# Expert 0's rows by one-hot products instead of a gather, in a mixer and MoE layer on one core

## The reference

```python
p_group = softmax(hf @ rg_w + rg_b)
g_prob, g_idx = top_k(p_group, 1)
top_p, top_i = top_k(softmax(sel), 2)
w = g_prob * top_p / sum(top_p)
for e in range(16):
    y = (silu(h @ w_gate[e]) * (h @ w_up[e])) @ w_down[e]
    out = out + combine[:, e:e + 1] * y
```

## Time and profile before

| | us |
|---|---|
| median of 3 runs | 552.3 (551.95 to 555.5) |
| the profiled execution | 552.4 |
| its span (first to last instruction) | 550.6 |
| TensorE busy in the span | 536.9 |
| VectorE / ScalarE / GpSimd busy | 421.3 / 353.3 / 91.3 |

### The profile page before, as it was taken

One profiled execution on the slowest core, in us unless ns is written; L12 is line 12 of the kernel. 1 busy time (PEld: TensorE's weight loads), 2 busy tenths in 40 slices (PEclk: granted clock), 3 DMA queues, 4 the chain that ended last, 5 costly groups with the idle time before them and its releaser, 6 DMA issues.

```text
span 550.6 us, 7873 instructions
## 1 busy us (share of the span) xinstructions
PE 536.9 (98%) x2662; PEld 438.5 (80%) x2663; DVE 421.3 (77%) x580; ACT 353.3 (64%) x470; POOL 91.3 (17%) x113
## 2 busy tenths in 40 slices
PE   7999999999999999999999999999999999999995
PEld 5988777777877888877788888888888888888883
DVE  5654599554864753588989898988989898988986
ACT  5563654780326253355778978788778978788745
POOL 3260000000000000031412222022212222110420
PEclk9999999999999999999999999999999999999998
DMA  8999122323020237639999999999999999999796
GB/s 322 371 283 401 42 71 77 76 79 77 0 77 0 78 114 251 234 138 313 349 380 373 379 394 382 367 371 376 392 352 374 375 390 373 376 390 393 251 208 212
DMA packets 63821, 144.03 MB, mean 262 GB/s; under 512 B 3833, under 2 KB 13361, under 8 KB 63665
## 3 DMA queue, kind: packets, MB, share of 16 engines
q1 hardware_dynamic: 56528, 120.24, 61.4%
q0 software_dynamic: 7120, 22.90, 13.7%
q10 hardware_dynamic: 144, 0.52, 0.3%
HBM read 132.77 MB, written 14.30 MB: 267 GB/s over the span
## 4 chain that ended last, share of the span: by engine, by line
PE 88%; DVE 5%; ACT 2%; DMA 2%; issue 1%; POOL 0%; DVEq 0%; POOLq 0%
PE ps L1495 25%; PE ps L1497 24%; PE ps L1496 24%; PE ps L1502 7%; PE ps L1646 2%; PE ps L1632 2%; PE ps L1608 1%; PE ps L1578 1%; PE ps L1673 1%; DMA arena<-h_dram,meta 1%; DMA arena<-norm_g 1%; DVE lo_ring L1305 1%; DVE act_lo L1015 1%; PE ps L1896 1%; DVE res L1474 0%
## 5 line engine op out<-in xcount | busy, mean ns | idle before, releaser
L1305 DVE TENSOR_TENSOR lo_ring<-arena,hi_ring 128x2048 fp32r<-128x2048 f32 x94 | 213.8, 2288 | 26.9 <-ACT hi_ring L894 26.8
L1495 PE MATMUL ps<-hi_ring,act_hi 128*128 128x512 f32 x576 | 229.8, 399 | 1.5 <-DVE lo_ring L1305 1.1
L1497 PE MATMUL ps<-hi_ring,act_lo 128*128 128x512 f32 x576 | 224.9, 390 | 0.0
L1496 PE MATMUL ps<-lo_ring,act_hi 128*128 128x512 f32 x576 | 224.4, 390 | 0.0
L894 ACT ACTIVATE hi_ring<-arena 128x2048 fp32r<-128x2048 f32 x94 | 180.2, 1917 | 28.1 <-PE ps L1497 28.1
L1495 PEld LDWEIGHTS ps<-hi_ring,act_hi 128*128 128x128 f32 x576 | 108.3, 188 | 23.5 <-issue 2.4
L1497 PEld LDWEIGHTS ps<-hi_ring,act_lo 128*128 128x128 f32 x576 | 108.1, 188 | 23.3
L1496 PEld LDWEIGHTS ps<-lo_ring,act_hi 128*128 128x128 f32 x576 | 108.4, 188 | 20.9
L1005 DVE SCALAR_TENSOR_TENSOR lo_ring<-arena,over,hi_ring 128x512 fp32r<-128x512 f32 x40 | 29.2, 747 | 29.4 <-ACT hi_ring L708 29.2
L1015 DVE TENSOR_TENSOR act_lo<-ps,act_hi 128x512 fp32r<-128x512 f32 x56 | 36.7, 683 | 7.6 <-ACT act_hi L742 5.6
L600 POOL DMA_INDIRECT arena<-h_dram,gather_idx x14 | 34.7, 2478 | 24.0 <-issue 24.0
(11 more groups left out here) (237 smaller groups left out, 523.0 us busy)
## 6 DMA issues: line engine op xcount, KB each, us to landing
arena<-w_gate SPq DMA_DIRECT2D x32, 1024.0 KB, 16.6
arena<-w_up SPq DMA_DIRECT2D x32, 1024.0 KB, 17.6
arena<-w_down SPq DMA_DIRECT2D x32, 1024.0 KB, 15.2
arena<-w_in SPq DMA_DIRECT2D x16, 512.0 KB, 7.2
y_dram<-arena POOLq DMA_DIRECT2D x8, 512.0 KB, 11.2
res<-y_dram POOLq DMA_DIRECT2D x8, 512.0 KB, 9.8
arena<-w_in SPq DMA_DIRECT2D x2, 1024.0 KB, 10.9
arena<-w_out SPq DMA_DIRECT2D x4, 512.0 KB, 6.5
```

Source lines behind the costliest of these rows:

```text
L1305: nc.vector.tensor_tensor(lo(N1 + n12), raw(n12), hi(N1 + n12).bitcast(F32), ALU.subtract).then_inc(lo_done, 1)
L1495: nc.tensor.matmul(dst, a_hi, b_hi, start=start, stop=False)
L1496: nc.tensor.matmul(dst, a_hi, b_lo, start=False, stop=False)
L1497: return nc.tensor.matmul(dst, a_lo, b_hi, start=False, stop=stop)
```

## The change

The normed tiles get homes of their own in SBUF (`h2_home`) and stay there. VectorE compares each token's rank in expert 0 with the row numbers (`find_first`), and TensorE multiplies each normed tile with that one-hot (`first_rows`): four f32 matmuls for each tile and half, summed over the four tiles in banks 4 and 5, which gives expert 0's rows turned. These take the place of expert 0's list, gather and transposes, and of the fillers. The lists are still made, for the other experts: GpSimd's first gathers are now those of experts 1 and 2, behind the last one-hot product, since two of the tiles lie in `x_rows`. The list's weights are made behind the first two products instead of before them. Differences and sums for the routing weights move from VectorE to GpSimd. Lengths, slots and flags move into VectorE's steps of experts 0 and 1. The two `y_buf` change places, so that `route` lies over `y_buf[1]`; ScalarE waits for the flags before expert 1's scaled rows instead of before the first silu. GpSimd waits for the lengths before its gather of expert 3. SyncE's loads 8 to 10 wait for the last h2 tile and the two turned halves.

```diff
-y_buf = [nc.alloc_sbuf_tensor_at("y0", [P, D], F32, offset=at_hi + 2560 * 4),
-         nc.alloc_sbuf_tensor_at("y1", [P, D], F32, offset=at_lo + 2560 * 4)]
+y_buf = [nc.alloc_sbuf_tensor_at("y0", [P, D], F32, offset=at_lo + 2560 * 4),
+         nc.alloc_sbuf_tensor_at("y1", [P, D], F32, offset=at_hi + 2560 * 4)]
...
-h2_buf = [region(O_XG, D), region(O_XG + D, D)]
+x_rows = [region(O_XG, D), region(O_XG + D, D)]
+h2_home = [region(O_BIAS, D), region(O_BIAS + D, D), x_rows[1], x_rows[0]]
+first_hot = region(O_BIAS + 2 * D, T * P).rearrange("p (t s) -> p t s", t=T)
...
-route = y_buf[0][:, 0:1024]
+route = y_buf[1][:, 0:1024]
...
-        if n == RING2 - 4:
-            sp.wait_ge(rows_in[0], 16)
+        if n == O_BIAS // GRAN - 1:
+            sp.wait_ge(h2_out[T - 1], 16)
+        elif n == O_BIAS // GRAN:
+            sp.wait_ge(x_turned, 1)
+        elif n == O_BIAS // GRAN + 1:
+            sp.wait_ge(x_turned, 2)
...
-        pool.dma_start(h2_dram[t * P:(t + 1) * P, :], h2_buf[t % 2]).then_inc(h2_out[t % 2], 16)
+        pool.dma_start(h2_dram[t * P:(t + 1) * P, :], h2_home[t]).then_inc(h2_out[t], 16)
...
+    pool_steps = [0]
...
+    def pool_done(ins):
...
+    g_top, g_exp = route[:, 472:472 + T], route[:, 848:864].rearrange("p (t j) -> p t j", t=T)
+    diff = route[:, 400:400 + T * E].rearrange("p (t g j) -> p t g j", t=T, g=N_GROUPS)
+    pool_done(nc.gpsimd.tensor_tensor(diff.rearrange("p t g j -> p (t g j)"), route[:, 704:768], route[:, 640:704], ALU.subtract))
+    pool_done(nc.gpsimd.tensor_tensor(diff, diff, lg[:, :, 1:, :], ALU.mult))
+    nc.gpsimd.tensor_tensor(g_exp, lg[:, :, 0, :], g_top.unsqueeze(2).to_broadcast([P, T, 4]),
+                            ALU.subtract).then_inc(pool_step, 1)
+    pool_steps[0] += 1
+    folded = diff.rearrange("p t g j -> p t (g j)")
+    for n in (8, 4, 2):
+        pool_done(nc.gpsimd.tensor_tensor(folded[:, :, 0:n], folded[:, :, 0:n], folded[:, :, n:2 * n], ALU.add))
+    nc.gpsimd.tensor_tensor(route[:, 864:868].unsqueeze(2), folded[:, :, 0:1], folded[:, :, 1:2], ALU.add).then_inc(gate_d, 1)
...
-    for b in range(2):
-        pool.wait_ge(h2_out[b], 16 * T // 2)
+    for t in range(T):
+        pool.wait_ge(h2_out[t], 16)
     pool.wait_ge(lists_ready, 1)
-    for b in range(2):
-        pool.indirect_dma_start(x_rows[b], None, h2_dram, bass.IndirectOffsetOnAxis(ap=meta[:, 4 * b:4 * b + 1], axis=0),
-                                bounds_check=last_token, oob_is_err=False).then_inc(rows_in[b], 16)
+    pool.wait_ge(x_turned, 2)
+    for e in (1, 2):
+        pool.indirect_dma_start(x_rows[e % 2], None, h2_dram, bass.IndirectOffsetOnAxis(ap=meta[:, 4 * e:4 * e + 1], axis=0),
+                                bounds_check=last_token, oob_is_err=False).then_inc(rows_in[e % 2], 16)
     pool.dma_start(gain2, bass.AP(final_g.tensor, 0, [[0, P], [1, D]])).then_inc(gain_in, 16)
-    pool.wait_ge(info_made, 1)
+    pool.wait_ge(lengths_made, 1)
...
     def gather(b, e):

         nc.gpsimd.tensor_copy(gather_idx[:, b:b + 1], meta[:, bass.ds(e * 4, 1)]).then_inc(idx_ready, 1)
-        pool.wait_ge(idx_ready, e - 1)
...
-    pool.wait_ge(x_turned, 2)
-    pool.wait_ge(rows_in[0], 16)
-    gather(0, 2)
     pool.wait_ge(y_zeroed, 16 * 2 * T)
     pool.wait_ge(x_turned, 4)
     pool.wait_ge(rows_in[1], 16)
     gather(1, 3)
+    pool.wait_ge(info_made, 1)
     for e in range(2):
         traffic(e, e, True, False)
...
-    act.wait_ge(gate_d, 1)
-    nc.scalar.activation(route[:, 848:868], route[:, 848:868], ACT.Exp).then_inc(gate_e, 1)
-    nc.scalar.activation(stat[:, 47:48], eps[:, 0:1], ACT.Silu)
...
         if not first:
             act.wait_ge(y_sent[b], e * 8 - 8 * b)
+        elif b:
+            act.wait_ge(over_set, 1)
...
     split(2, 2, 16)
-    rows_hi(0, 1)
+    nc.scalar.activation(stat[:, 46:47], eps[:, 0:1], ACT.Exp)
+    rows_hi(0, 1, (0,))
+    act.wait_ge(gate_d, 1)
+    nc.scalar.activation(route[:, 848:868], route[:, 848:868], ACT.Exp).then_inc(gate_e, 1)
+    rows_hi(0, 1, (1,))
+    nc.scalar.activation(stat[:, 47:48], eps[:, 0:1], ACT.Silu)
     split(3, 3, 16)
-    act.wait_ge(over_set, 1)
     act.wait_ge(mm_done, used_value(N1 + 1))
     nc.scalar.activation(silu_g[:, :], ps[:, 0, :], ACT.Silu).then_inc(silu_ready, 1)
...
-            act.wait_ge(y_sent[0], 16 * (E // 2 - 1))
+            act.wait_ge(y_sent[1], 16 * (E // 2 - 1))
...
-        if t >= 2:
-            dve.wait_ge(h2_out[t % 2], 16)
-        nc.vector.scalar_tensor_tensor(h2_buf[t % 2], res_t[:, t, :], rms[:, T + t:T + t + 1], gain2,
+        nc.vector.scalar_tensor_tensor(h2_home[t], res_t[:, t, :], rms[:, T + t:T + t + 1], gain2,
...
         nc.vector.tensor_scalar(pair_any[:, t0 * E:t1 * E], flat, 2.0, None, ALU.is_lt).then_inc(pair_ready, 1)
+        if t1 == T:
+            nc.vector.tensor_reduce(g_top, lg[:, :, 0, :], AX_X, ALU.max)
...
+    def find_first(t0, t1, ahead):
+
+        last = t1 == T
+        step_done(nc.vector.tensor_scalar(miss[:, t0:t1], standing[:, t0:t1, 0, 0], 2.0, 2.0 * S, ALU.is_ge, ALU.mult))
+        dve.wait_ge(rank_ready, 2 if last else 1)
+        step_done(nc.vector.tensor_tensor(first_rank[:, t0:t1], ahead, miss[:, t0:t1], ALU.add))
+        for t in range(t0, t1):
+            nc.vector.tensor_scalar(first_hot[:, t, :], order, first_rank[:, t:t + 1], None,
+                                    ALU.is_equal).then_inc(first_hot_set, 1)
...
+    find_first(0, EARLY, ps[:, 1, 0:EARLY * E:E])
     find_ranks(0, EARLY, ps[:, 1, 0:EARLY * E])
-    mark(0)
     norm2(T - 1)
     gate(EARLY, T)
-    mark(1)
+    find_first(EARLY, T, ps[:, 2, 0:(T - EARLY) * E:E])
     find_ranks(EARLY, T, ps[:, 2, 0:(T - EARLY) * E])
-    for t in range(EARLY, T):
+    for t in range(T):
         mark(t)
+    nc.vector.tensor_copy(count, ps[:, 2, (T - EARLY) * E:(T - EARLY + 1) * E])
+
+    rows_lo(0, 1, (0,))
+    for piece in range(2):
+        split_piece(N1 + 1, piece)
+    rows_lo(0, 1, (1,))
     dve.wait_ge(lists_made, 1)
     nc.vector.tensor_scalar(meta_v[:, :, 0:2], ps[:, 7, 0:2 * E].rearrange("p (e f) -> p e f", f=2), float(NO_ROW),
                             None, ALU.add).then_inc(lists_ready, 1)
-
-    step_done(nc.vector.tensor_reduce(g_top, lg[:, :, 0, :], AX_X, ALU.max))
-    nc.vector.tensor_tensor(g_exp, lg[:, :, 0, :], g_top.unsqueeze(2).to_broadcast([P, T, 4]), ALU.subtract)
-    step_done(nc.vector.tensor_tensor(top_diff, pair_hot[:, 1, :], pair_hot[:, 0, :], ALU.subtract))
-    diff_tiles = top_diff.rearrange("p (t g j) -> p t g j", t=T, g=N_GROUPS)
-    step_done(nc.vector.tensor_tensor(diff_tiles, diff_tiles, lg[:, :, 1:, :], ALU.mult))
-    nc.vector.tensor_reduce(ratio, top_diff.rearrange("p (t e) -> p t e", t=T), AX_X, ALU.add).then_inc(gate_d, 1)
-    for piece in range(4):
+    for piece in range(2, 4):
         split_piece(N1 + 1, piece)
-    step_done(nc.vector.tensor_copy(count, ps[:, 2, (T - EARLY) * E:(T - EARLY + 1) * E]))
-    step_done(nc.vector.tensor_scalar(quarters, count, float(QUARTER), None, ALU.is_gt))
-    for i in (2, 3):
-        step_done(nc.vector.scalar_tensor_tensor(quarters, count, float(QUARTER * i), quarters,
-                                                 ALU.is_gt, ALU.add))
-    nc.vector.tensor_copy(meta_v[:, :, 3:4], quarters.unsqueeze(2))
+
     dve.wait_ge(gate_e, 1)
...
-    rows_lo(0, 1)
     split(2, 2)
+    split(3, 3)
...
+    def set_lengths():
+        step_done(nc.vector.tensor_scalar(quarters, count, float(QUARTER), None, ALU.is_gt))
+        for i in (2, 3):
+            step_done(nc.vector.scalar_tensor_tensor(quarters, count, float(QUARTER * i), quarters,
+                                                     ALU.is_gt, ALU.add))
+        nc.vector.tensor_copy(meta_v[:, :, 3:4], quarters.unsqueeze(2)).then_inc(lengths_made, 1)
+
+    def set_slots():
...
+        step_done(nc.vector.scalar_tensor_tensor(place_kt, rank_kt, float(E), place_kt, ALU.mult, ALU.add))
...
+    def set_flags():
+        for i in range(1, S // P):
+            ins = nc.vector.tensor_scalar(flags[0][:, (i - 1) * E:i * E], count, float(P * i), None, ALU.is_gt)
+        step_done(ins)
+        nc.vector.tensor_copy(over[:, 0:UNITS], flags[0])
+        step_done(nc.vector.memset(over[:, UNITS:UNITS + 1], 0))
+
+    def sum_flags(shifts):
+
+        for shift in shifts:
+            cur = (shift.bit_length() - 1) % 2
+            a, b = flags[cur], flags[1 - cur]
+            nc.vector.tensor_copy(b[:, 0:shift], a[:, 0:shift])
+            step_done(nc.vector.tensor_tensor(b[:, shift:], a[:, shift:], a[:, 0:UNITS - shift], ALU.add))
+
...
+    def step(b, e, last=False, first=False):
         for c in range(PER_E):
             split(e * PER_E + 4 + c, (4 + PER_E * b + c) % RING2)
+            if first and c == 0 and b == 0:
+                rows_lo(1, 3)
+            if first and c == 0 and b:
+                set_flags()
+            if first and c == 2 and b:
+                sum_flags((1, 2, 4))
```

(94 more changed lines are left out.)

27 lines of the change are left out of this document (18 added, 9 removed).

## The result

| | before | after |
|---|---|---|
| median, us | 552.2 (4 runs) | 559.4 (4 runs, 559.2 to 560.7) |
| profiled execution / its span, us | 552.4 / 550.6 | 559.5 / 557.8 |
| mean granted clock of the span | 0.996 | 0.988 |

What follows compares the result with a forecast made beforehand. TensorE was taken to bound the expert loop, a wait chain the handover. Terms -4.0 (front), +3.6 (GpSimd's queue), +0.7 and +3.1 (flags) summed to +3.4 on 552.4: forecast 555.8 us, range 550.5 to 560.0.

Steps and rivals of the forecast that it cites:

- front part, hidden rows of expert 0: Up to expert 0's hidden rows being turned: at 263.1 instead of 267.05, -4.0 us, bounds -5.2 and -1.5.
- ScalarE's wait for GpSimd's copy: Before expert 0's scaled rows: ScalarE stands 4.1 us until GpSimd copies row numbers and weights at 276.0.
- TensorE's loss behind it: TensorE holes one weight split after ScalarE's two waits: 3.6 us after GpSimd's copy, 3.1 us after the flags.
- flags between expert 1's first splits: Five small VectorE operations there make hidden rows 0.7 us late, bounds 0 and 0.8.
- ScalarE's wait for the flags: Before expert 1's scaled rows: ScalarE stands 3.5 us until the last seven flag operations end at 297.0.
- clock: Rival, chance 0.25: clock falls in the new TensorE holes; 558.5 with one slow product behind one hole, 561.3 behind each.
- Handover: From late rank matmuls to first expert products: one-hot products replace list, gather and fillers; first product at 246.6, not 251.04.
- then the first product: 246.6: Handover's last step: late ranks at 241.1, one-hot calls 4.45, list products 1.04, first product at 246.6 instead of 251.04.
- The 0.6 us kept for expert 1's gather: Expert 1's rows, needed at 255.8, were taken to land at 256.4, 0.6 us late; bounds 0 and 2.1.
- GpSimd's chain: GpSimd's queue in expert 0's step: lengths, gathers for experts 3 and 4, then the copy; costs TensorE 3.6, bounds 0.5 and 4.0.
- 266.5 + 4.65 + 4.68 + 0.2: Lengths ready, expert 3's gather, expert 4's gather, then the copy of row numbers and weights, done at 276.0.
- Flags: Eighteen small VectorE operations moved into the steps of experts 0 and 1: 0.7 us late rows, 3.1 us of TensorE.

Runs made afterwards that it cites:

- e1: The changed kernel with the lists' lengths made by VectorE before its second weight split instead of in expert 0's step: 553.2 us.
- e7: The changed kernel with both ScalarE waits removed, plus the first expert product waiting only for its own weight block: 548.1 us, 0.9 below the same without this edit.
- e4: The changed kernel with GpSimd's copy of expert 0's row numbers and weights put ahead of its wait for the lengths and two gathers: 552.5 us.
- e6: The changed kernel with VectorE's fourth to sixth split of expert 0's step cut into four instructions each: 555.3 us.

## Why the prediction was right in direction and short in size

Forecast 555.8, measured 559.4: inside the range, on its upper side, slower by 1.2%.

| step | forecast | measured |
|---|---|---|
| front part, hidden rows of expert 0 | -4.0 | -3.4 |
| ScalarE's wait for GpSimd's copy | 4.1 | 6.10 |
| TensorE's loss behind it | +3.6 | +5.7 |
| flags between expert 1's first splits | +0.7 | 0 (0.4 in e1) |
| ScalarE's wait for the flags | 3.5 | 3.36 |
| TensorE's loss behind it | +3.1 | +2.9 |
| clock | 0 in the forecast | +1.9 |
| sum | +3.4 | +7.2 |

*Handover.* The one-hot products cost what the retention rows said: from 241.03 to 245.53. The step that failed is "then the first product: 246.6": it came at 247.98, because its semaphore counts pieces of the next block too. I had listed what must be ready and left that count unread; e7 gives 0.9 us of it back. The 0.6 us kept for expert 1's gather was not needed, but only because the first product was late: the rows were issued at 248.21, landed 7.9 us later at 256.10, and were asked for at 257.18 where the forecast had 255.8. So two errors offset each other, and that the front part came within 0.6 us is partly luck. The bounds written out for this part add up to -1.3 us on the late side, not -1.5, and do not reach -5.2 on the other. One reading was wrong without effect: ScalarE's wait of at most 0.8 us in the loop holds for the weights' high parts; for the hidden rows it waits up to 1.24 us.

*GpSimd's chain.* The place, the queue order and the releaser were right, and e4 shows the mechanism directly. The term was mis-sized at 3.6, and its upper bound of 4.0 was broken. "266.5 + 4.65 + 4.68 + 0.2" became 267.14 + 6.51 + 4.93 + 0.20: the lengths 0.6 late with the front, the first gather 1.9 longer. The 4.65 stands in no row; in the trace of before expert 3's gather took 4.42 (copy from 260.51, issued at 264.93). The two copies alone took 3.4 us more than two of 0.55; the second issue, 1.00 us with VectorE idle where the same place in the trace of before had 2.55 (270.72 to 273.27), gave 1.6 of that back by luck. I took the copy's price from a row where it began 0.5 us before the split beside it ended. The earlier trace rows had it: the copy from 268.59 took 0.55 us and ended at 269.14, the split from 266.81 ended at 269.09. A copy that starts with a split pays the whole split. The Trainium skill (SBUF — State Buffer, section Who interferes with whom) says that a VectorE instruction with two inputs in SBUF contends with a GpSimd instruction that reads SBUF, and that the order of issue decides which of two blocks the other. The traces agree, with GpSimd's copy the later one: 2.17 and 2.31 us beside whole splits, 0.57 and 0.61 beside split pieces in e6, and 0.18 in e1 at 258.90, where VectorE worked on an input from PSUM.

*Flags.* Right in place and size: over at 301.27, and with the net delay of what stands before, 7.64 - 3.37 = 4.27, taken off that is 297.0, as forecast. The 0.7 between expert 1's first splits didn't show, since the product at the lower clock ended later (288.99) than the hidden rows were ready (287.57); without that it is 0.4 (e1).

*Clock.* This was a rival with a chance of 0.25, and it came true behind the first hole; its time for that, 558.5, was the nearest of all that were named, though its terms were off by 2.7 us one way (front, GpSimd's chain) and 1.7 the other (flags, clock). I had one product lose 2.73; it lost 1.93, since the clock rose again before its last matmuls. The Trainium skill (TensorE: Matmul & The Clock Gate, section What's actually happening) says that throttled is the default; the hole of 5.30 us agrees, and the second hole, kept at 1.00 in this profile, shows that the rule doesn't say by itself which hole pays.

The profile's test that the prediction set, a granted clock under 1.00 between 275 and 310, was the one that told against the forecast; a wait of 6.1 instead of 4 us was the second.

## What to carry to other kernels

When a producer moves later, price what is queued behind its waiter on every engine, and put what another engine needs soon ahead of what nobody needs yet: moving one copy in GpSimd's queue was worth as much as making the lengths early (552.5 and 553.2). Small operations belong where the trace shows the engine idle, by place and not by the sum of idle time: the same eighteen flag operations cost 3 us in one place and nothing in another. Read the number that each wait compares with before you say when a moved instruction can start.
